# A two-layer transformer kernel on one core: head-norm weights moved into the copies after the transposes, engine orders rewritten

## The reference, cut to what matters

```python
def head_layernorm(y, g, n_heads):
    ...
    mu = jnp.mean(yf, axis=-1, keepdims=True)
    var = jnp.mean(jnp.square(yf - mu), axis=-1, keepdims=True)
    yn = ((yf - mu) * lax.rsqrt(var + EPS)).reshape(B, S, W)
    return yn * g.astype(jnp.float32)
...
        y_m = (jax.nn.sigmoid(mo.astype(f32)) * head_layernorm(hm, m_norm_g[i], M_HEADS)).astype(dt)
...
        y_r = (jax.nn.silu(rg.astype(f32)) * head_layernorm(hr, r_norm_g[i], R_HEADS)).astype(dt)
        merged = jax.nn.sigmoid(gm) * (y_m @ w_bm[i]) + jax.nn.sigmoid(gr) * (y_r @ w_br[i])
        x = x + merged @ w_out[i]
```

## Time and profile before

| | |
|---|---|
| median of 3 runs | 3228.33 us (3226.37 to 3233.46) |
| profiled execution: first to last instruction | 3219.8 us, 8.5 us under the median; that much lies around it |
| PE busy | 3150.0 us, 98% of the span |
| DVE, ACT, POOL busy | 66%, 47%, 15% |
| mean granted PE clock | 0.992 |
| first block | from 0 to about 1282 us |

### The profile page before, as it was taken

One profiled execution on the slowest core, in us unless ns is written; L12 is line 12 of the kernel. 1 busy time (PEld: TensorE's weight loads), 2 busy tenths in 40 slices (PEclk: granted clock), 3 DMA queues, 4 the chain that ended last, 5 costly groups with the idle time before them and its releaser, 6 DMA issues.

```text
span 3219.8 us, 49381 instructions
## 1 busy us (share of the span) xinstructions
PE 3150.0 (98%) x20586; PEld 2790.3 (87%) x20586; DVE 2121.0 (66%) x3125; ACT 1500.2 (47%) x1717; POOL 485.0 (15%) x276
## 2 busy tenths in 40 slices
PE   8999999999999999989999999999999999999998
PEld 8797889797978897878999989888769999999887
DVE  6775665577767655676967755555688767655555
ACT  6444454564444544613444444444445444444443
POOL 0000000000000000000866600000004766200000
PEclk9999999999999999999999999999999999999999
DMA  6454645444546454404554465555524544565553
GB/s 231 154 198 162 222 171 196 171 146 169 198 161 215 181 196 152 179 2 155 183 178 152 148 257 200 190 191 195 183 79 171 181 162 144 220 223 188 193 195 131
DMA packets 87944, 565.12 MB, mean 176 GB/s; under 512 B 10224, under 2 KB 10240, under 8 KB 23856
## 3 DMA queue, kind: packets, MB, share of 16 engines
q1 hardware_dynamic: 80784, 534.81, 46.3%
q0 software_dynamic: 6944, 27.21, 2.5%
HBM read 552.54 MB, written 9.44 MB: 175 GB/s over the span
## 4 chain that ended last, share of the span: by engine, by line
PE 54%; DVE 4%; ACT 1%; issue 0%; DVEq 0%; ACTq 0%
PE bank L2150 22%; PE bank L2177 7%; PE bank L2181 7%; PE bank L2176 7%; PE bank L2131 4%; PE bank L2115 0%; DVE w_lo L2613 0%; PE bank L1845 0%; ACT w_hi L2330 0%; PE bank L1842 0%; PE bank L1841 0%; PE bank L1813 0%; PE bank L1808 0%; PE bank L1809 0%; PE bank L1830 0%
## 5 line engine op out<-in xcount | busy, mean ns | idle before, releaser
L2613 DVE TENSOR_TENSOR w_lo<-raw,w_hi 128x2048 fp32r<-128x2048 f32 x224 | 514.8, 2299 | 344.3 <-ACT w_hi L2330 343.4
L2330 ACT ACTIVATE w_hi<-raw 128x2048 fp32r<-128x2048 f32 x291 | 555.7, 1910 | 335.3 <-PE bank L2150 264.8
L1057 DVE TENSOR_TENSOR w_lo<-raw,w_hi 128x2048 fp32r<-128x2048 f32 x200 | 458.1, 2292 | 314.8 <-ACT w_hi L818 313.1
L818 ACT ACTIVATE w_hi<-raw 128x2048 fp32r<-128x2048 f32 x201 | 384.9, 1917 | 438.9 <-PE bank L548 237.3
L2150 PE MATMUL bank<-act_hi,w_hi 128*128 128x256 f32 x2048 | 489.6, 282 | 0.0
L2150 PE MATMUL bank<-act_lo,w_hi 128*128 128x256 f32 x2048 | 485.0, 280 | 0.0
L2150 PEld LDWEIGHTS bank<-act_hi,w_hi 128*128 128x128 f32 x2048 | 385.9, 188 | 0.2
L2150 PEld LDWEIGHTS bank<-act_lo,w_hi 128*128 128x128 f32 x2048 | 386.0, 188 | 0.0
L2176 PE MATMUL bank<-w_hi,c_hi 128*128 128x512 f32 x992 | 385.9, 389 | 0.0
L2177 PE MATMUL bank<-w_hi,c_lo 128*128 128x512 f32 x992 | 385.9, 389 | 0.0
L1697 POOL TENSOR_TENSOR w_lo<-raw,w_hi 128x2048 fp32r<-128x2048 f32 x68 | 313.5, 4615 | 168.2 <-ACT w_hi L2330 168.0
(11 more groups left out here) (562 smaller groups left out, 5287.0 us busy)
## 6 DMA issues: line engine op xcount, KB each, us to landing
raw<-weights SPq DMA_DIRECT2D x492, 1024.0 KB, 4.8
row<-rows POOLq DMA_DIRECT2D x48, 256.0 KB, 4.3
spill<-staged SPq DMA_DIRECT2D x32, 256.0 KB, 2.8
hid<-spill SPq DMA_DIRECT2D x32, 256.0 KB, 5.0
y<-w_pe POOLq DMA_DIRECT2D x2, 1024.0 KB, 5.0
ln_row_mix<-ln_rows POOLq DMA_DIRECT2D x4, 512.0 KB, 5.3
hid<-keys POOLq DMA_DIRECT2D x2, 1024.0 KB, 6.3
ln_row_ffn<-ln_rows POOLq DMA_DIRECT2D x4, 512.0 KB, 7.8
```

The costliest lines, as they stand in the source:

```text
L818: nc.scalar.activation(w_hi[:, k % SPLIT, :], raw[:, k % RAW, :], ACT.Copy).then_inc(hi_ready, 1)
L1057: nc.vector.tensor_tensor(w_lo[:, k % SPLIT, :], raw[:, k % RAW, :], w_hi[:, k % SPLIT, :].bitcast(F32), ALU.subtract).then_inc(lo_ready, 1)
L2330: A.activation(hi_of(k), raw[:, k % RAW, :], ACT.Copy).then_inc(hi_ready, 1)
L2613: V.tensor_tensor(lo_of(k), raw[:, k % RAW, :], hi_of(k).bitcast(F32), ALU.subtract).then_inc(lo_ready, 1)
```

## The change

The weight multiplications of `gating` go (12 instructions to a layer). The weights are loaded once, at the start, as columns `gains` (one value per partition, 12 transfers of 512 single values for both layers), and a new `gained` on ACT and on DVE applies them as a per-partition scale while copying the transposed banks, 128x256 at a time where `mixed` took 128x512; `mixed` stays for the later projection. The rows ring has 18 rows to a layer where it had 24. The identity products at the four places named above (9 to a layer) are dropped, the others stay. The orders of DVE and ACT around both mixers are rewritten.

```diff
+ROW_AT = []
+GAIN_AT = []
+_r = 0
...
-        ROW_CHUNK += [CHUNK[_name, _i]] * (1 + _gains)
-ROWS_A = len(ROW_CHUNK)
-
-GAIN_ROWS = {ROW_OF[_name, _i] + 1: _n + _i + 1 for _name, _n, _of in (("mo", 0, 2), ("rg", 2, 4)) for _i in range(_of)}
+        ROW_CHUNK.append(CHUNK[_name, _i])
+        ROW_AT.append(_r)
+        if _gains:
+            GAIN_AT.append(_r + 1)
+        _r += 1 + _gains
+ROWS_A = _r
+ROWS_USED = len(ROW_CHUNK)
...
+    gains = sb("gains", [P, LAYERS, GAINS], F32, memory)
...
-                for r in range(ROWS_A):
-                    if layer and r < RROW:
...
+                for r in range(ROWS_USED):
+                    n = layer * ROWS_USED + r
+                    if n >= RROW:
+                        wait_read(pool, ROW_CHUNK[(n - RROW) % ROWS_USED], (n - RROW) // ROWS_USED)
...
-                    pool.dma_start(row[:, r % RROW, :], rows[layer, r].partition_broadcast(P)).then_inc(row_loaded[r % RROW], 16)
+                    pool.dma_start(row[:, n % RROW, :], rows[layer, ROW_AT[r]].partition_broadcast(P)).then_inc(row_loaded[n % RROW], 16)
+                    if n == RROW - 1:
+                        for at in range(LAYERS):
+                            for i, source in enumerate(GAIN_AT):
+                                pool.dma_start(gains[:, at, i * KB:(i + 1) * KB], rows[at, source].rearrange("(k p) -> p k", p=P),
+                                               allow_slow_non_contiguous=True).then_inc(gains_loaded, 16)
...
-        def row_slot(name, i, k=0):
-            r = ROW_OF[name, i] + k
-            return row[:, r % RROW, :], row_loaded[r % RROW], 16 * (r // RROW + 1)
+        def row_slot(name, i, layer):
+            n = layer * ROWS_USED + ROW_OF[name, i]
+            return row[:, n % RROW, :], row_loaded[n % RROW], 16 * (n // RROW + 1)
...
-                def nat(name, i, hi, lo, ready=None, tiles=None, half=None, warmth=0):
+                def nat(name, i, hi, lo, ready=None, tiles=None, half=None):
                     if tiles is None or 0 in tiles:
                         bank_free(CHUNK[name, i])
-                        warm(2 * (CHUNK[name, i] % 2), warmth)
...
-                    warm(4, warmth)
                     outputs(3)
...
-                       lambda i, j: nat("mo", i, act_hi, act_lo, tiles=(j,)), warmth=2)
+                       lambda i, j: nat("mo", i, act_hi, act_lo, tiles=(j,)))
                 nat("gm", 0, act_hi, act_lo)
-                nat("gm", 1, act_hi, act_lo, tiles=(0,), warmth=3)
+                nat("gm", 1, act_hi, act_lo, tiles=(0,))
                 pe.wait_ge(y_ready, 2 + layer * A_LAYER["y_ready"])
                 transposes(lambda k, t: y[:, t, k * P:(k + 1) * P], KD)
                 nat("gm", 1, act_hi, act_lo, tiles=(1,))
-                nat("bm", 0, mix_hi, mix_lo, Mixed(M_YM), warmth=1)
+                nat("bm", 0, mix_hi, mix_lo, Mixed(M_YM))
...
-                nat("rg", 3, act_hi, act_lo, warmth=3)
+                nat("rg", 3, act_hi, act_lo)
...
+
+                def gained(first, k0, gain):
+
+                    for b in range(KD // 2):
+                        act.wait_ge(trans_done, first + b + 1 + layer * A_LAYER["trans_done"])
+                        for k in (2 * b, 2 * b + 1):
+                            ins = nc.scalar.activation(mix_hi[:, k0 + k, :], psum[4 + b][:, (k % 2) * S:(k % 2 + 1) * S], ACT.Copy,
+                                                       scale=gains[:, layer, gain + k:gain + k + 1])
+                            do(ins, t_hi) if k % 2 else do.also(ins)
...
-                def gates(name, i, func, dst, src=None):
-                    stream(name, i)
+                def gate_of(name, i, func, dst, src):
                     wait_read(act, CHUNK[name, i], layer)
-                    do(nc.scalar.activation(dst, pre[:, :, :] if src is None else src, func), gated)
+                    do(nc.scalar.activation(dst, src, func), gated)
 
                 for i in range(2):
+                    stream("mo", i)
                     held = merged[:, :, i * CW:(i + 1) * CW]
-                    gates("mo", i, ACT.Sigmoid, held, held)
+                    gate_of("mo", i, ACT.Sigmoid, held, held)
                 head_std(1)
-                gates("gm", 0, ACT.Sigmoid, gate[:, :, 0:CW])
-                mixed(T_YM, 0)
-                gates("gm", 1, ACT.Sigmoid, gate[:, :, CW:D])
+                if layer == 0:
+                    act.wait_ge(gains_loaded, 16 * LAYERS * len(GAIN_AT))
+                stream("gm", 0)
+                split_hi(base, TILE["bm", 0])
+                gate_of("gm", 0, ACT.Sigmoid, gate[:, :, 0:CW], pre[:, :, :])
+                gained(T_YM, 0, GAIN_M)
+                split_hi(base, TILE["bm", 0] + 1)
+                gate_of("gm", 1, ACT.Sigmoid, gate[:, :, CW:D], pre[:, :, :])
...
+                head_std(2)
+                split_hi(base, TILE["rg", 3])
                 held_gate(1)
-                head_std(2)
-                for i in range(2, 4):
-                    gates("rg", i, ACT.Silu, pre[:, :, :])
-                gates("gr", 0, ACT.Sigmoid, gate[:, :, 0:CW])
-                mixed(T_YR, 0)
-                gates("gr", 1, ACT.Sigmoid, gate[:, :, CW:D])
-                mixed(T_YR + 4, KD)
+                split_hi(base, TILE["rg", 3] + 1)
+                split_hi(base, TILE["gr", 0])
+                gate_of("rg", 2, ACT.Silu, pre[:, :, :], pre[:, :, :])
+                split_hi(base, TILE["gr", 0] + 1)
+                gate_of("rg", 3, ACT.Silu, pre[:, :, :], pre[:, :, :])
+                stream("gr", 0)
+                gate_of("gr", 0, ACT.Sigmoid, gate[:, :, 0:CW], pre[:, :, :])
+                gained(T_YR, 0, GAIN_R)
+                stream("gr", 1)
+                gate_of("gr", 1, ACT.Sigmoid, gate[:, :, CW:D], pre[:, :, :])
+                gained(T_YR + 4, KD, GAIN_R + KD)
...
-                def gating(name, i, count, held):
-
-                    g = row_of(name, i, 1)
-                    for t in range(TT):
-                        do.also(V.tensor_tensor(y[:, t, i * CW:(i + 1) * CW], y[:, t, i * CW:(i + 1) * CW], g, ALU.mult))
-                    do.settle()
+                def gating(i, count, held):
+
                     dve.wait_ge(gated, count + layer * A_LAYER["gated"])
                     for t in range(TT):
                         ys = y[:, t, i * CW:(i + 1) * CW]
@@ -1238,26 +1272,29 @@
                 first_tile = TILE["mo", 0]
                 m_weigh(0)
                 m_weigh(1)
-                split_lo(base, first_tile + SPLIT)
                 m_output(0)
                 m_weigh(2)
+                split_lo(base, first_tile + SPLIT)
+                gate_in("mo", 0, merged[:, :, 0:CW])
+                m_output(1)
+                m_weigh(3)
                 split_lo(base, first_tile + 1 + SPLIT)
-                m_output(1)
-                gate_in("mo", 0, merged[:, :, 0:CW])
-                m_weigh(3)
+                m_output(2)
                 split_lo(base, first_tile + 2 + SPLIT)
-                m_output(2)
-                split_lo(base, first_tile + 3 + SPLIT)
                 gate_in("mo", 1, merged[:, :, CW:D])
                 m_output(3)
+                split_lo(base, first_tile + 3 + SPLIT)
                 head_norm(1, MDV)
                 split_lo(base, TILE["gm", 0] + SPLIT)
-                gating("mo", 0, 1, merged[:, :, 0:CW])
+                gating(0, 1, merged[:, :, 0:CW])
+                gating(1, 2, merged[:, :, CW:D])
                 split_lo(base, TILE["gm", 0] + 1 + SPLIT)
-                gating("mo", 1, 2, merged[:, :, CW:D])
                 gate_in("gm", 0, pre)
-                mixed(M_YM, 0)
-                stream("gm", 1)
+                split_lo(base, TILE["bm", 0])
+                if layer == 0:
+                    dve.wait_ge(gains_loaded, 16 * LAYERS * len(GAIN_AT))
+                gained(M_YM, 0, GAIN_M)
+                split_lo(base, TILE["bm", 0] + 1)
                 dve.wait_ge(gated, 3 + layer * A_LAYER["gated"])
                 gate_in("gm", 1, pre)
...
+                r_output(3)
                 gate_in("rg", 1, gate[:, :, CW:D])
-                r_output(3)
                 head_norm(2, RDV)
-                for i in range(2, 4):
-                    split_lo(base, TILE["rg", i] + SPLIT)
-                    gating("rg", i - 2, 4 + i - 1, gate[:, :, (i - 2) * CW:(i - 1) * CW])
-                    split_lo(base, TILE["rg", i] + 1 + SPLIT)
-                    if i == 3:
-                        gating("rg", 2, 4 + 3, pre)
-                    gate_in("rg", i, pre)
-                gating("rg", 3, 4 + 4, pre)
+                split_lo(base, TILE["rg", 3])
+                gating(0, 5, gate[:, :, 0:CW])
+                split_lo(base, TILE["rg", 3] + 1)
+                gating(1, 6, gate[:, :, CW:D])
+                gate_in("rg", 2, pre)
+                split_lo(base, TILE["gr", 0])
+                gating(2, 7, pre)
```

(7 more changed lines are left out.)

29 lines of the change are left out of this document (17 added, 12 removed).

## The result

The changed kernel takes 3188.44 us (median of 4 runs, 3187.53 to 3191.78) against 3230.18 us (median of 4, 3226.37 to 3233.46) for the kernel before: ratio 0.9889, 95% interval 0.9873 to 0.9905. The forecast was 3200.4 with a range of 3195 to 3212. The sign is right, the time lies 6.6 us under the range. Three executions among all that follow, at 3506.5, 3922.6 and 5802.1 us with a mean granted clock of 0.75 to 0.85, count in no ratio. The profiled execution took 3187.93 us, its span is 3186.1 us: 33.7 us under the span of before, where the sum said 27.9.

What follows compares the result with a forecast made beforehand. PE was taken as the bound, busy 3150.0 of 3219.8 us. M mixer 18.4 and R mixer 11.45, less 2.0 for a new wait at br0, made 27.9 us; 3228.3 - 27.9 = 3200.4, range 3195 to 3212.

Steps and rivals of the forecast that it cites:

- (a): M mixer, PE between tile mo1.1 and outputs(3): two identity products and the idle before DVE's division go, 2.85 us a layer.
- (b): M mixer, PE between gm0.1 and gm1.0: three identity products go, 2.60 us a layer.
- (c): M mixer, PE between gm1.0's last eight matmuls and the transposes: the wait for y goes, 2.87 us a layer.
- (d): M mixer, PE from the identity product before bm0 to L530: 0.88 us a layer goes.
- R: R mixer, PE: three products before rg3, 2.60 us, and the wait before the transposes, 2.30, go; layer 0 regains 1.65 half clock.
- The new wait at the third tile of br0: R mixer: longer scaled copies on ACT make PE wait about 1.0 us a layer, 2.0 in all.
- The transfers: Twelve startup loads of 512 values: 6144 packets, 71 us on 16 engines, both ends hidden, so 0 cost.
- rival 3: Single-value transfers land late, ACT and PE stop before gm1.0's split; at 0.5 us a packet 3273 us; chance 0.03.
- (1): Late DVE or ACT orders put waits in the dropped products' place; only 12.3 us gained, time 3216; chance 0.13.
- (2): As (1), and the clock falls behind six longer waits, 1.7 us each; time 3226; chance 0.03.
- (4): The forecast gain with a luckier clock and no wait at br0: 31 to 34 us, 3194 to 3197; chance 0.11.
- my own case: The summed gains in both mixers hold, giving 3197 to 3205 us; chance 0.70.

## Why the prediction was wrong

**The size of the change was right.** The sum was 27.9 us and the end of the first block moved by 27.9. Term by term, from the steps of the timelines (layer 0). One row of the timeline of PE before is needed beside the earlier trace rows, the start of outputs(2):

```profile
118.68 0.59 PE L718 MATMUL bank<-val,weighed 128*128 128x257 f32 x2
```

- (a) 2.85 forecast. From outputs(2) to outputs(3) are 128.40 - 121.59 = 6.81 us, and 128.34 - 118.68 = 9.66 before, so 2.85 less. Right, and the new order of DVE with the products gone is why: with the products alone dropped the wait grows, with the weights alone moved it stays.
- (b) 2.60 and (c) 2.87: measured 2.60 and 4.70 - 1.84 = 2.86. (d) 0.88: from the transposes to L540 are 155.29 - 146.21 = 9.08 us, 10.03 before, so 0.95. Together 9.26 for 9.20.
- R: 2.60 and 2.30 forecast. 333.39 - 331.56 = 1.83 for 4.13 before is 2.30, and the products' step gave 2.59 (8.08 before, 5.49 now). The half clock came back, 1.65.
- bm0 began at 153.46, not near 150.6. This was a matter of the start: the stretch at 0.50 near 30 us lasted 10.2 us for 6.8, and a second one came at 74. Together with what else differs, PE reached the M mixer 121.59 - 118.68 = 2.9 us later, and 6.8 instead of 10.2 us at 651 gave 1.7 of it back. The prediction allowed 3.5 each way for this.
- The new wait at the third tile of br0 cost 0.5 us a layer, not 1.0 (the tile takes 5.91 us from start to start and the one ahead of it 5.44; the list of waits counts 0.2 of it as idle). Eight scaled copies of 471 ns take 3.46 us in a row, 0.43 apiece, since each starts before the one ahead of it has ended. I had added a gap of 0.03 to each and come to 4.0. This term was mis-sized by 0.5, twice. With the measured terms the sum is 2 x 9.26 + 2 x 4.89 + 1.65 - 0.9 = 29.0; the luck of the clock at the two starts, 2.9 lost and 1.7 won, took 1.2 away again, so that a sum equal to the tenth is partly chance.
- The transfers: the twelve are issued in 9.7 us, and they land 20.2 us after their issue, in the median, by the DMA issues of the trace:

```profile
gains<-rows POOLq DMA_DIRECT2D x12, 2.0 KB, 20.2
```

The queue carried 6368 packets where it carried 6944. That is 576 packets fewer for twelve row loads less and twelve of these more. Between 40 and 140 us the queue carried four row loads and nothing else, in 320 packets, so a row load is 80 packets and twelve are 960: the transfers are 960 - 576 = 384 packets, 32 for each, and not 6144. Nothing waits for them. Zero was right, the bound of 71 us was far too wide, and rival 3 had no basis. Of each 32 packets 16 carry 128 bytes, that is 32 of the values, and 16 carry 4 bytes. The page "DMA: Bandwidth & Descriptors" of the Trainium skill says, under Rules for kernel authors, that a strided last dimension lowers to one descriptor per element. The trace counts packets and not descriptors, so no run here shows it or speaks against it. My error was to take each descriptor for a packet of its own: the count of 6144 does not follow from that rule.

**The step that failed** is the last of the prediction's sum: "The median lies 8.5 above the span, so the time is 3228.3 - 27.9 = 3200.4 us." I took the difference between the span of one execution and the median of others for time around the span. Every profiled execution here shows 1.8 us around it (3187.93 and 3186.1, 3216.93 and 3215.1, 3193.66 and 3191.9, 3224.03 and 3222.2). The other 6.7 were that the profiled execution of before was quicker than all of the runs shown. Its own time by that rule was 3219.8 + 1.8 = 3221.6, and 3221.6 - 27.9 = 3193.7 is the forecast which the working supported. It was to be seen beforehand: the three runs shown spread over 7 us, so a gap of 8.5 to one of their kind could not be read as a fixed cost.

**What lies beyond.** Even 3193.7 is 5 us above 3188.4. The means over all unchanged profiles give 30.1 us for the first block, 2.2 more than the sum. 1.1 of it is the wait at br0, and 0.5 is clock: that the half clock behind a wait is drawn anew each time is shown by the last two profiles of before, and the prediction counted the one stretch that the profiled execution had, 1.65 us, where the mean is 2.1. The rest is within what one profile differs from the next. 2.6 us of the means are in the second block, and may be chance. The two comparisons of before and after on one chip that followed gave 33.3 and 31.8 us between the medians, and the means of the spans give 32.6.

The first comparison gave 41.7, because its four executions of before are at 3226 to 3233, while in every later comparison the median of before is 3219 to 3222. The changed kernel was at 3188 everywhere. **These 8 us stay open.** The pace of the long streams doesn't explain them: with breaks in the streams the kernel before doesn't become faster. A lead in the record is the clock. In the 63 later executions of the kernel before that count, the time goes with the mean granted clock (correlation -0.59): the five at 0.990 average 3225.7 us, the thirteen at 0.993 average 3218.8. In the 14 of the changed kernel there is no such link (-0.11). The clocks of the first four executions of before are not on record, so that more half clock made them slow is possible and not shown. What was not tried is a profile of an execution of before that takes 3230.

**The rivals.** (1), waits in the products' place, is refuted in the changed kernel; it is what happens when the products alone are dropped, in part at least. (2) is seen there too: behind the longer waits the clock falls. (4), 3194 to 3197 by a luckier clock and no wait at br0, was nearer than my own case, though for reasons of which it named half.

## What to carry to other kernels

Filler work ahead of a wait had no net price here while the wait was there (what dropping it won, the lower clock took back) and its full price once the wait was gone, so measure it in the new order, not in the old. When two edits only pay together, neither carries the gain: run the combinations before naming one. Work the sum out against the profiled execution's own time, and place that execution among the other runs before adding its gap to their median: the gap is luck, not overhead. Removing a wait removes also the chance of a slow clock behind it, which one profile can't price.

## What the runs showed of the hardware that was not expected

- Long streams of 128x256 matmuls run at one of two paces, 113.3 or 117.8 ns from start to start, with a granted clock of 1.00 in both. A stream of 1152 keeps its pace to the end, 130.5 or 135.6 us (28 streams, 6 of them slow); at one of 30 inserted 16-column products the pace changed, and each costs 0.23 us. What chooses the pace was not found.
- Near 30 us the stretch at a granted clock of 0.50 lasted 6.8 us in some executions and 10.2 in others of the same kernel, 1.7 us of difference. Behind waits for y of 2.1 to 2.7 us the clock fell to 0.50 for 3.4 us in some executions and stayed at 1.00 in others.
- Twelve transfers that gather 512 single values over 128 partitions each are 384 packets. POOL needs 0.81 us to issue one. They land after 20.2 us. At that time, the kernel's start, the four broadcast rows of 256 KB issued just ahead of them also take 17.6 us, where a row takes 4.4 in the median of all, so the 20.2 can't be put down to the shape of the transfers.
